# Two layers with 32 routed experts each: the last weights in another order, and expert 29 finished before expert 30 starts

## The reference, cut to what matters

```python
def hierarchical_moe(t, wg, bg, we, be, w1, w3, w2):
    ...                                            # router: top-1 group, top-2 experts in it
    combine = jnp.sum(jax.nn.one_hot(expert_id, N_EXPERTS) * top_w[..., None], axis=1)

    def add_expert(acc, p):
        w1_e, w3_e, w2_e, c_e = p                  # (1024, 256), (1024, 256), (256, 1024)
        hidden = jax.nn.silu(t @ w1_e) * (t @ w3_e)
        return acc + c_e[:, None] * (hidden @ w2_e), None
```

## Time and profile before

| what | value |
|---|---|
| median of 3 runs | 1040.85 us (1040.86, 1038.17, 1040.85) |
| span of the profiled execution, first to last instruction | 1037.2 us |
| that execution's own time beside it | not listed; the median lies 3.65 us above the span, the shortest run 0.97 us |
| TensorE busy | 964.0 us, 93% of the span |
| mean granted clock of TensorE | 0.987 |
| VectorE, ScalarE, POOL busy | 35%, 24%, 21% |
| moved | 315.90 MB, 305 GB/s on the mean |
| largest wait of TensorE for weights | ring<-in_moe_w, 22.2 us in 18 waits |
| layer 0's experts | about 352 to 596 us |
| layer 1's experts | about 793 to 1031 us |

### The profile page before, as it was taken

How to read it: one execution, slowest core, us unless ns; L and a number is a source line. 1 busy time by engine, 2 the same in 40 slices (tenths; PEclk the granted TensorE clock), 3 DMA queues, 4 the chain that set the end, 5 groups by cost and what they waited for, 6 DMA issues and landing times.

```text
span 1037.2 us, 17822 instructions
## 1 busy us (share of the span) xinstructions
PE 964.0 (93%) x6167; PEld 612.2 (59%) x6168; DVE 359.3 (35%) x835; ACT 248.9 (24%) x538; POOL 212.6 (21%) x306
## 2 busy tenths in 40 slices
PE   5999999998998799998998899999998999998896
PEld 3444458545887455555555384877886555555652
DVE  4159494554346211110001271136435212222124
ACT  5110002444324122221212250022223111111112
POOL 1008400110000243332332000000003333332310
PEclk9999999999999899998999999999999999999999
DMA  9984545999806699999999989264647998999996
GB/s 355 316 269 169 191 141 207 313 334 381 340 20 227 241 370 406 405 406 406 408 406 407 355 293 351 82 234 137 199 160 272 399 401 303 406 406 404 403 405 253
DMA packets 129081, 315.90 MB, mean 305 GB/s; under 512 B 28891, under 2 KB 59891, under 8 KB 128996
## 3 DMA queue, kind: packets, MB, share of 16 engines
q1 hardware_dynamic: 113200, 295.93, 76.7%
q0 software_dynamic: 10800, 12.72, 3.6%
q10 hardware_dynamic: 4996, 6.09, 1.6%
HBM read 315.07 MB, written 22.31 MB: 325 GB/s over the span
## 4 chain that ended last, share of the span: by engine, by line
PE 72%; DMA 14%; issue 3%; DVE 3%; ACT 3%; SPq 2%; POOL 1%; ACTq 0%; POOLq 0%; DVEq 0%
PE ps L1137 17%; PE ps L941 16%; DMA ring<-in_moe_w 11%; PE ps L993 8%; PE ps L1163 8%; PE ps L951 5%; PE ps L895 3%; PE ps L1109 2%; SPq L709 2%; PE ps L1296 1%; DMA RH<-hrow,sidx_all 1%; PE ps L1147 1%; PE ps L929 1%; PE ps L1347 1%; PE ps L1475 1%
## 5 line engine op out<-in xcount | busy, mean ns | idle before, releaser
L1137 PE MATMUL ps<-ring,RT 128*64 128x256 f32 x2128 | 256.9, 394 | 25.0 <-DMA ring<-in_moe_w 22.2
L1137 PEld LDWEIGHTS ps<-ring,RT 128*64 128x64 f32 x2128 | 162.9, 141 | 94.8 <-issue 25.3
L941 PE MATMUL ps<-RT,ring 128*128 128x512 f32 (+1 forms) x544 | 182.0, 493 | 0.5 <-DVE RT L2333 0.5
L941 PEld LDWEIGHTS ps<-RT,ring 128*128 128x128 f32 x544 | 102.2, 190 | 76.5 <-issue 69.8
L2220 DVE TENSOR_TENSOR RT<-RT,ps 64x256 f32<-64x256 f32 x64 | 27.0, 422 | 268.2 <-ACT RT L1729 268.2
L1163 PE MATMUL ps<-ring,RT 128*64 128x512 f32 x424 | 100.5, 593 | 1.4 <-DVE RT L2226 1.0
L1729 ACT ACTIVATE RT<-ps 64x256 f32<-64x256 f32 x64 | 24.2, 377 | 252.8 <-PE ps L1137 252.8
L2375 DVE SCALAR_TENSOR_TENSOR RAB<-RM,chan,RAB 128x512 f32<-128x512 f32 x120 | 79.7, 749 | 0.0
L2624 POOL DMA_INDIRECT pair_out<-RH,sidx_all x62 | 62.9, 1015 | 55.5 <-POOL sidx_all L2621 52.7
L2600 POOL DMA_INDIRECT RH<-hrow,idx x7 | 8.1, 1155 | 306.6 <-DVE idx L2172 192.4
L2612 POOL DMA_INDIRECT RH<-hrow,sidx_all x56 | 59.2, 1057 | 49.4 <-POOL sidx_all L2609 49.4
(11 more groups left out here) (290 smaller groups left out, 1002.7 us busy)
## 6 DMA issues: line engine op xcount, KB each, us to landing
ring<-in_moe_w SPq DMA_DIRECT2D x358, 512.0 KB, 14.4
ring<-in_w_mod SPq DMA_DIRECT2D x96, 512.0 KB, 9.5
ring<-in_odd_w_in SPq DMA_DIRECT2D x24, 512.0 KB, 9.6
ring<-in_even_w_in SPq DMA_DIRECT2D x20, 512.0 KB, 10.0
ring<-in_even_w_out SPq DMA_DIRECT2D x8, 512.0 KB, 11.3
RAB<-in_moe_w SPq DMA_DIRECT2D x8, 512.0 KB, 7.9
RAB<-pair_out SPq DMA_DIRECT2D x8, 512.0 KB, 6.7
ring<-in_odd_w_out SPq DMA_DIRECT2D x8, 512.0 KB, 4.2
```

The costliest lines, as they stand in the source:

```text
L941: mm = pe.matmul(bank, w[:, c, P * ft:P * (ft + 1)], moving[:, c, :], start=(c == 0), stop=(c == NCH - 1))
L1137: mm = pe.matmul(bank[CAP * k:CAP * (k + 1), 0:BLK], xt(c), w[k][:, BLK * c:BLK * (c + 1)], start=(c == 0), stop=(c == NCH - 1))
```

## The change

The weights are asked for in the same order up to the third last expert. Then `w2` of expert 29 comes ahead of `w1` and `w3` of expert 30, where it came behind them. On TensorE the last steps are written out: `Dn` of expert 29 stands ahead of `U` of expert 30, so that `U` of expert 30 is followed directly by `Hd` of expert 30, the constant products and `U` of expert 31. ScalarE, VectorE and POOL follow: copying out expert 29's result and scattering it stand ahead of expert 30's work. Both layers use the same code.

```diff
+    last = EXPERTS - 1
+    for e in range(last - 1):
         yield from ((e, 0), (e, 1))
         if e:
             yield e - 1, 2
+    yield last - 2, 2
+    yield from ((last - 1, 0), (last - 1, 1), (last, 0), (last, 1), (last - 1, 2), (last, 2))
...
+                def last_steps(counts):
...
+                    step(i, 0, counts[0])
+                    late_slots()
+                    step(i, 1, counts[1])
+                    T(i, 3)
+                    Hd(i, 1)
+                    Dn(i, 1)
+                    used(i, 1, (2,))
+                    idle()
+                    U(i, 2)
+                    more(i, 2, counts[2])
+                    used(i, 2, (0, 1))
+                    Hd(i, 2)
+                    idle()
+                    U(i, 3)
+                    more(i, 3, counts[3])
+                    used(i, 3, (0, 1))
+                    Dn(i, 2)
+                    used(i, 2, (2,))
+                    Hd(i, 3)
+                    Dn(i, 3)
+                    used(i, 3, (2,))
...
+                def last_two(counts):
...
+                    copy_xT(i, 3)
+                    if l == 0:
+                        copy_y(i, 1)
+                    silu(i, 2)
...
                 for q in range(PER_LOOP):
+                    if q == 2:
+                        scatter(LAST_GROUP, 1)
                     more(LAST_GROUP, q, counts[q])
                     if q + 1 < PER_LOOP:
                         ahead(LAST_GROUP, q + 1, counts[q + 1])
-                    if q + 1 < PER_LOOP:
+                    if q < 2:
                         scatter(LAST_GROUP, q - 1)
```

More of the change, by code:

```diff
@@ L292, in order_of_use @@
 def order_of_use():
-    for e in range(EXPERTS):
+    last = EXPERTS - 1
+    for e in range(last - 1):
         yield from ((e, 0), (e, 1))
@@ L297, in order_of_use @@
             yield e - 1, 2
-    yield EXPERTS - 1, 2
+    yield last - 2, 2
+    yield from ((last - 1, 0), (last - 1, 1), (last, 0), (last, 1), (last - 1, 2), (last, 2))
 IN_RING = {l: [w for w in order_of_use() if w not in SPARE[l]] for l in (0, 1)}
@@ L1194, in used, with step @@
                     free(sum(not isinstance(i, int) or (PER_LOOP * i + q, k) not in SPARE[l] for k in ks))
-                def step(i, q, count, ahead=True):
-                    if ahead:
-                        T(*job_after(i, q, 1))
+                def step(i, q, count):
+                    T(*job_after(i, q, 1))
                     Hd(i, q - 1)
[L1201 to L1205, removed]
                     U(i, q)
@@ L1212, in step, with idle @@
                     used(i, q - 1, (2,))
+                def last_steps(counts):
+                    i = LAST_GROUP
+                    def idle():
+                        pe.wait_ge(x_y_ready, pe.snap(extras))
+                        for _ in range(2):
+                            pe.matmul(ps[:, 7, 0:BLK], ident, const[:, 0:BLK], start=True, stop=True)
+                    step(i, 0, counts[0])
[19 more added lines that the diff above has]
+                    used(i, 3, (2,))
                 def late_slots():
@@ L1267, in experts @@
                         step(i, q, c[q])
[L1268 to L1275, removed]
+                last_steps(extra_counts(pe, l, LAST_GROUP))
                 late_results()
@@ L1756, in more, with one @@
                                 act.activation(YSX, bank, ACT.Copy).then_inc(x_y_ready, 1)
-                def one(i, q, count, ahead=True):
-                    if ahead:
-                        copy_xT(*job_after(i, q, 1))
+                def one(i, q, count):
+                    copy_xT(*job_after(i, q, 1))
                     silu(i, q)
@@ L1764, in one @@
                         copy_y(i, q - 1)
+                def last_two(counts):
+                    i = LAST_GROUP
+                    copy_xT(i, 3)
+                    if l == 0:
+                        copy_y(i, 1)
+                    silu(i, 2)
+                    more(2, counts[2])
+                    silu(i, 3)
+                    more(3, counts[3])
+                    if l == 0:
+                        copy_y(i, 2)
+                        copy_y(i, 3)
                 if l == 1:
@@ L1783, in experts @@
                 late_slots()
[L1784 to L1787, removed]
+                one(LAST_GROUP, 1, c[1])
+                last_two(c)
                 table(ACT.Sqrt)
@@ L2284, in experts @@
                 late_slots()
-                for q in range(PER_LOOP):
+                for q in (0, 1):
                     one(LAST_GROUP, q, c[q])
-                copy_hT(LAST_GROUP, PER_LOOP - 1)
+                copy_hT(LAST_GROUP, 1)
                 if l == 1:
-                    gated_y(LAST_GROUP, PER_LOOP - 1)
+                    gated_y(LAST_GROUP, 1)
+                for q in (2, 3):
+                    hidden(LAST_GROUP, q)
+                    more(q, c[q])
+                    if q == 2:
+                        copy_hT(LAST_GROUP, q)
+                if l == 1:
+                    gated_y(LAST_GROUP, 2)
+                copy_hT(LAST_GROUP, 3)
+                if l == 1:
+                    gated_y(LAST_GROUP, 3)
             def late_pair(l):
```

## The result

| what | before | changed |
|---|---|---|
| median of 6 runs | 1040.28 us (1038.17 to 1042.8) | 1046.4 us (1045.35 to 1050.01) |
| span of the profiled execution | 1037.2 us | 1043.8 us |
| mean granted clock of TensorE | 0.987 | 0.983 |

The ratio is 1.0071, with a 95% interval of 1.0054 to 1.0088. The forecast was 1040.2 us in a range up to 1042.2; the time lies 4.2 us above that range. The profiled execution took 1045.55 us, 1.75 above its span.

The account below looks back on a forecast made before the run. The weights' stream was taken to set the pace, leaving only the layers' tails to move. Terms +0.8 - 0.3 - 1.2 = -0.7 us took 1040.85 to about 1040.2 us, range 1037.7 to 1042.2.

Parts of the forecast that it names:

- step 1: Weights' stream: expert 29's w2 comes 5.3 us earlier, expert 31's weights unchanged, ring places return in the new order; no cost.
- Rival E: Change doesn't do what it says, expert 29's w2 still late, pushing expert 30: +0.5 to +1; chance counted in B's.
- step 6: Layer 0's end: earlier request for the rows gains 1.2 us (0 to 1.7), kept through layer 1's mixer and first experts.
- Step 2: Expert 29's down projection, 4.2 us earlier, fits into TensorE's waits ahead of expert 30's up projection; cost 0.
- Step 3: Nothing covers the gap behind expert 30's up projection, so expert 31's starts 0.8 us later (0 to 1.3).
- Steps 4 and 5: Expert 29's scatter and SP's row request come 4.2 us earlier; in layer 1 worth -0.3 us, layer 1 in sum +0.5.
- rival A: Layer 0's rows come back much earlier, giving 1.7 us there; sum -1.2 to -2.0, 1038.9 to 1039.7; chance 0.15.
- the paragraph behind the sum: Skill page's DMA cost: layer 0's four transfers, 2 MB, in 7 us; layer 0 gains 1.7, sum -1.2; trace disagrees.
- B: Layer 0 gains nothing because gate rows hold the queue, layer 1 pays: +0.5 to +1.0, 1041.4 to 1041.9; chance 0.20.
- C: Early row request delays expert 31's w2 at the layers' ends: about +2.9 or more, 1043.7 to 1046.2; chance 0.05.
- D: TensorE's clock falls at the new gap, expert 31's up projection at half clock in both layers: +2.2, 1043.1; chance 0.05.

Follow-up runs that it names:

- e1: Changed kernel with the constant products carrying the due ring-place return, in both layers; 1037.52 us against 1038.97 of the kernel before, ratio 0.9987.
- e7: Changed kernel, return kept, without the constant products ahead of expert 31's up projection in both layers; 1036.04 us against 1037.94 of the kernel before, ratio 0.9984.
- e6: Changed kernel, return kept, new order in layer 1 only, layer 0 as before; 1038.39 us against 1037.94 of the kernel before, ratio 1.0014.
- e2: Kernel before, old order, with layer 0's return for expert 30's w2 left out; 1046.29 us against 1038.97 of the kernel before, ratio 1.0070.
- e5: Changed kernel, return kept, new order in layer 0 only, layer 1 as before; 1036.00 us against 1037.94 of the kernel before, ratio 0.9982.
- e8: Changed kernel, return kept, expert 30's Hd put into the middle of expert 31's up projection; 1036.10 us against 1037.94 of the kernel before, ratio 0.9982.
- e9: New order in layer 0 only, return kept, without constant products ahead of expert 31 there; 1037.08 us against 1039.43 of the kernel before, ratio 0.9979.
- e3: Changed kernel with the return kept in layer 0 only, still lost in layer 1; 1038.75 us, ratio 0.9994 to the kernel before.
- e4: Kernel before, old order, with layer 0's returns for w2 of experts 29 and 30 left out; 1051.71 us, ratio 1.0114 to the kernel before.

## Why the prediction was wrong

**The step that failed is step 1**: "The ring's places come back in the new order too, and the requests that a later return could hold up were all made 12 places earlier: no cost." One place does not come back at all. Its price, about 7 us, is larger than every term of the sum, and it falls due not at the changed place but some 170 us later, from 741 us on, when layer 1's experts are fetched ahead. I had asked when the return comes, and never whether the instruction that carries it is run. **Rival E** was dismissed wrongly too: "The orders on SP and TensorE show that it does." They show which instructions stand where; which semaphore an instruction raises, and by how much, they don't show, and that was all that differed. The closing sentence of step 6, that the first experts of layer 1 "all shift alike", fell with step 1; in e1, with the return kept, experts 0 to 2 start 2.4, 1.9 and 1.9 us earlier than before.

By its own steps, apart from that:

- *Step 2* holds: the down projection stands ahead of expert 30's up projection, which still waits for its weights, 0.52 us in place of the predicted 0.4.
- *Step 3* holds: 1015.39 - 1009.29 = 6.10 us predicted between the two up projections, 6.09 in the changed kernel and 6.11 in e1. Some of that agreement is luck: the turning starts 4.69 us behind expert 30's up projection (4.59 predicted), and from there to expert 31's it takes 1.40 us (1.51). From expert 29's up projection to expert 31's it takes 16.45 us, where it took 15.79: +0.7 for the predicted +0.8. Without the products (e7) the distance is 5.59, so they make up 0.5 of it.
- *Steps 4 and 5* hold: in layer 1 the earlier request is worth the 0.3 us of the first group, 2.29 to 1.98. Layer 1 in sum was forecast at +0.5; e6 gives +0.4 by its medians and +1.5 by its ratio (0 to +3.0 us), the traces +0.3 to +0.4.
- *Step 6* was probably undersized. I took -1.2 and set **rival A**, 1.7, beside it. The trace of the changed kernel looks like rival A: 383 GB/s at a share of 1.04, VectorE without a wait. From expert 29's up projection to the next mixer it takes 601.01 - 559.76 = 41.25 us, where it took 604.50 - 561.60 = 42.90: 1.65 less. But two executions of the old order (e2, e6) take 40.5 and 40.9 us for this stretch, so the 1.65 is one pair of traces. e5 measures -1.9 us (-0.6 to -3.2), which leaves the -1.2 possible too. The share of 0.89 at 294 GB/s, in which I saw engines held up, is full once the request is earlier. SP asked for the rows at 577.51, against 582.99 before; step 6 had 578.8. The four transfers then landed 9.4 us after their issue on the median (8.1 before), each later than the 7 us that the paragraph behind the sum worked out for all four.
- *Rivals B, C and D*: B is excluded by e5. C did not happen: from expert 31's up projection to the end of the span it takes 22.3 us in the changed kernel and in e1, 22.6 before. D: the half clock at expert 31 came in none of the new tails of layer 1 read (changed, e1, e6, e7, e8) and once in layer 0, in e9, where the products are left out. The 5.20 us at expert 1 in the changed kernel stand behind 3.81 us of idling that the missing place made.

Return kept, the change is worth 1.4 us (e1), against a forecast of 0.7. Both are below the 0.3% that the prediction set as the least that can be told from no change.

**What stays open.** That the missing place costs some at the first experts and some later (5.4 and 2.9 us between e1 and the changed kernel) is read from two traces, and wasn't tested apart. Why the second transfer from `pair_out` is late in some executions of the old order and not in others isn't known. So it stays open how much of e5's 1.9 us is that wait. How far the half-clock up projections in layer 1's stream (three behind expert 1 in the changed kernel, two before, one in e1) have a part in the later loss isn't shown either; e3 has three of them there and an expert 0 at half clock, and is as fast as the kernel before.

## What to carry to other kernels

Where a count to be given back is held over and attached to "the next suitable instruction", that instruction must be one that always runs: after any reordering, look at each place where a conditional body could take the count, and flush it ahead of the branch. Here the lost return stopped nothing and changed no instruction's place; it showed only as one place less, as a long wait of the requesting queue for one return, in the next layer. So when a small reordering at one place costs time at another, compare what the queues wait for, one by one, ahead of asking about the order itself. And an earlier request is worth what its consumer lacked: here about 2 us in layer 0, where TensorE and VectorE waited for the rows, and 0.3 us in layer 1, where TensorE needed them only later.

## What the hardware showed that I had not expected

- A gather by POOL's queue landed in 2.1 us in the kernel before (median of three), and its rows were turned only 6.7 us after its issue in the changed kernel. There the DMA share stood at 1.00 or more from 789 to 795 us; before, it fell to 0.52 at 793 and 0.07 at 794. That the backlog of SP's requests made the gather late is argued from this, and e2 with its own backlog agrees (3.32 us of idling at the same place).
- One place of twelve is worth a lot here: 12 places to 11 cost 0.70%, to 10 1.14% (e2, e4). It isn't bandwidth that is lost but time to fetch ahead: 50 GB/s in place of 141 over 30 us of the mixer, with the same 315.90 MB moved in all. Whether a thirteenth place would gain anything wasn't run.
- TensorE's clock is granted at full (1.00) over layer 0's end and ahead of layer 1's experts in both kernels; after the idle 3.81 us it was granted at 0.50, the 1.2 GHz level, until about 802 us, and the up projection in it took 5.20 us for 3.67. In e9 it was 0.50 behind 1.02 us of idling, 0.42 us of work and 1.04 us of idling; in e7 it stayed at 1.00 where the second wait was 0.35.
